# The products of the SSM output projection set among the halves of the paged attention, in a two-layer decoder step

## The chip, the cores and the metric

One NeuronCore of a Trainium2 chip runs the whole kernel. The metric is the time of the device for one execution, in microseconds (us); lower is better. The engines are PE (matmul), with its weight loads shown apart as PEld, DVE (vector), ACT (scalar), POOL (GpSimd) and SP (sync), whose queue issues most of the DMAs here. All data are float32.

## The reference

One inference step of a trunk with two layers: a prompt of 256 tokens and 8 sample tokens, each sample with 2048 tokens of cached context in 16 pages of 128, share the weights. Cut to what matters here, a layer is:

```python
h = rmsnorm(x); proj = h @ w_in         # gates, z, xBC, dt, c_q, c_kv, k_rope
# branch A (SSM): conv, chunked scan, gate with silu(z), grouped norm
ya = rmsnorm_grouped(y * silu(z)) @ w_ssm_proj          # the y projection
# branch B: latent attention; the samples' keys and values come from a page table
kv = cache_latent[l][page_table]; kr = cache_krope[l][page_table]
p  = softmax((q_lat @ kv.T + q_pe @ kr.T) * scale); o = p @ kv
yb = (o @ w_vb) @ w_mla_proj
x = x + (sigmoid(gate_a) * ya + sigmoid(gate_b) * yb) @ w_out
x = x + peer(rmsnorm(x, norm_ffn))      # product-key retrieval of experts
```

The y projection is 264 x 1024 by 1024 x 1024. The prompt's attention is causal, over 2 tiles of 128 tokens, 8 heads.

## The kernel before

A hardware loop runs two layers, each unrolled, with one instruction stream per engine. The order of the work is written out by hand on every engine, and semaphores tie the streams. PSUM is used as two rings of four banks: `wide` (banks 0 to 3, emptied mostly by ACT) and `aux` (4 to 7, emptied by DVE). PE fills banks in program order and DVE reads them in the same order, so both streams must list the pieces alike.

Weights stream through `wring`, two buffers of one block each. `load_block` on SP waits, for block n, until PE has begun block n-1 (semaphore `blocks_begun`), and PE's `next_block` waits for the block's landing. The y projection has 4 blocks of 256 columns (1 MB each); every block gives two outputs m of 128 features by 264 tokens, each a `product` of 8 chunks (L456). DVE multiplies each into `gate` (L1209).

The cached context of a sample comes in two halves of 8 pages, so there are 16 halves (`HALVES`). A page is 272 KB (128 partitions of 544 floats: latent turned, rotary key turned, latent). Three halves are held (`HELD`); slot 2 lies in room that the SSM work uses until `ring_free`. Ahead of the issue of each half, SP loads its eight page numbers from DRAM into registers (`half_numbers`, L1776: one load of the table's address and one of the numbers); `half_pages` (L1783) then issues eight DMAs. From half 3 on SP waits, after it has the numbers, for the values product of the half three before (`marks["values", i - HELD]`).

On PE each half is: `half_scores` (L772 and L776), the pieces of the prompt's attention that `PROMPT_PIECES` sets to this half, `half_turns` (L465, two transposes of the probabilities), `half_values` (L797). Between scores and turns DVE takes the maximum (L1251 to L1254) and ACT the exp (L1653); between turns and values DVE copies (L1259). The prompt's pieces are `prompt_scores(t, q)` (L738, L741), `prompt_turns` (transposed probabilities, copied by DVE into `pt`) and `prompt_values` (L760). DVE's `prompt_maxima` (L1225) and `prompt_probs` (L1233, which scales the probabilities by the sums) stand ahead of what follows them in its order, and ACT's exps of the prompt are set by `PROMPT_EXPS`.

All eight outputs of the y projection stand before half 0 on PE and DVE. On SP their blocks stand so: block 0 before the pages of half 1, block 1 after them and before the wait on `ring_free`, block 2 in the middle of half 2, block 3 after it, then the first block of w_mla, then the pages of halves 3 to 15, then the rest. `pt` lies in the room of `z`, which is also `yt`, the input of the y projection. The row `nrow` (1024 floats in each partition) holds the layer's first norm weight, used once; POOL reloads it with the second one (`norm_ffn`) after the state work, and DVE reads it for the norm ahead of the experts (L1344). POOL also loads and stores the SSM states of the samples (L1874, L1868); ACT scales them (L1626) in the stretch in which the gates' products run and SP issues halves 0 and 1.

## Time and profile before

| | |
|---|---|
| runs, median (lowest to highest of 3) | 2533.2 us (2532.52 to 2535.57) |
| profiled execution, its own time | 2528.51 us |
| its span, first to last instruction | 2527.0 us |
| mean granted TensorE clock | 0.944 of full |
| PE / DVE / ACT / POOL busy | 82% / 60% / 19% / 25% of the span |

The profile is of one execution. A page gives busy times, a span in slices and the costliest groups of instructions; the trace behind it can be asked for a timeline, for windows, for one line's instructions and for waits. A layer takes about half of the span; the page halves are the stretches from 327.75 to 451.40 us (layer 0) and from 1580.60 to 1700.80 us (layer 1). In a timeline, a row is a merged run of one line's instructions: start, length (from the first start to the last end), engine, line, operands, count, and in brackets the idle time of the engine before it and who ended it. PE's records count a product of float32 twice (x16 are eight products).

### The profile page before, as it was taken

The page shows a single profiled execution, that of the slowest core. Times are in us where ns is not written, and L with a number is a line of the kernel's source. Part 1 is how long each engine was busy: PE and PEld are TensorE (multiplying, and loading weights), DVE is VectorE, ACT ScalarE, POOL GpSimd, SP SyncE. Part 2 cuts the span into 40 slices and gives each one's busy share as a digit, 9 for nine tenths or more (in the row PEclk, how much of TensorE's full clock was granted, in tenths as well). Part 3 has the DMA queues.
Part 4 walks back from the last instruction along what each step waited for, and adds up shares of the span by engine and source line. Part 5 has one row for each costly group of instructions (what it writes and reads, how often), then busy time and mean ns, then how long its engine had stood idle before and what let it go on. Part 6 is the DMA issues. An engine that isn't in the chain of part 4 may idle for free. (4 is left out here: it accounts for less than half of the span.)

```text
span 2527.0 us, 26287 instructions
## 1 busy us (share of the span) xinstructions
PE 2067.5 (82%) x8858; PEld 1158.4 (46%) x8858; DVE 1518.1 (60%) x3811; ACT 477.2 (19%) x1458; POOL 633.3 (25%) x592
## 2 busy tenths in 40 slices
PE   6999777888888877787779988779879887777775
PEld 4886554654444322222258866446534343222222
DVE  2534423227878888888525343232387878888884
ACT  1226211001111111111122361110111111111111
POOL 0001000003343444444200010000043444444441
PEclk9999788889999999999979998789899999999998
DMA  5436368129999999999744273762399999999996
GB/s 158 149 97 216 125 222 271 56 82 377 424 422 409 427 385 427 427 427 427 332 146 155 92 237 119 235 227 84 100 425 423 424 412 427 380 427 427 426 425 268
DMA packets 201953, 740.27 MB, mean 293 GB/s; under 512 B 16274, under 2 KB 92490, under 8 KB 133696
## 3 DMA queue, kind: packets, MB, share of 16 engines
q0 software_dynamic: 83008, 581.14, 55.5%
q1 hardware_dynamic: 118800, 157.36, 19.3%
q8 instruction: 72, 1.18, 0.2%
q14 instruction: 73, 0.60, 0.1%
HBM read 727.17 MB, written 11.46 MB: 292 GB/s over the span
## 5 line engine op out<-in xcount | busy, mean ns | idle before, releaser
L915 PE MATMUL ps<-arena 128*128 128x512 f32 (+1 forms) x2112 | 1015.8, 615 | 258.7 <-DVE arena L1447 258.5
L1889 POOL DMA_INDIRECT arena<-in_peer_uv,arena x528 | 587.8, 1113 | 824.1 <-PE ps L915 695.4
L915 PEld LDWEIGHTS ps<-arena 128*128 128x128 f32 (+1 forms) x2112 | 365.6, 187 | 886.0 <-DVE arena L1447 576.8
L1438 DVE CUSTOM_DVE_ANT_0 arena<-arena,h 128x1024 f32<-128x1024 f32 x512 | 626.5, 1224 | 198.8 <-DMA arena<-in_peer_uv,arena 190.5
L456 PE MATMUL ps<-ht_tok,wring 128*128 128x264 f32 x1664 | 391.9, 392 | 6.7 <-DMA wring<-in_w_in 5.1
L456 PEld LDWEIGHTS ps<-ht_tok,wring 128*128 128x128 f32 x1664 | 316.5, 193 | 79.7 <-issue 15.4
L1710 ACT ACTIVATE arena<-arena 128x1 f32<-128x1 f32 x528 | 105.8, 202 | 1035.9 <-DVE arena L1438 1035.3
L1447 DVE TENSOR_SCALAR arena<-consts,arena 128x128 f32<-128x128 f32 (+1 forms) x528 | 181.8, 344 | 42.7 <-ACT arena L1710 42.0
L1880 POOL DMA_DIRECT2D arena<-in_peer_keyst x2 | 1.1, 552 | 539.7 <-PEq L862 539.7
L456 PE MATMUL ps<-arena,wring 128*128 128x264 f32 x384 | 89.7, 396 | 3.7 <-DMA wring<-in_w_ssm_proj 2.6
L456 PE MATMUL ps<-wring,gate 128*128 128x256 f32 (+1 forms) x384 | 87.1, 386 | 6.0 <-DVE gate L1328 6.0
L456 PEld LDWEIGHTS ps<-arena,wring 128*128 128x128 f32 x384 | 74.4, 195 | 18.4 <-DMA wring<-in_w_ssm_proj 3.5
L465 PE MATMUL ps<-consts,h 128*128 128x128 f32 (+2 forms) x166 | 42.6, 356 | 44.4 <-DVE h L1344 18.7
L456 PEld LDWEIGHTS ps<-wring,gate 128*128 128x128 f32 (+1 forms) x384 | 60.0, 160 | 32.9 <-DVE gate L1328 6.8
L465 PE MATMUL ps<-consts,arena 128*128 128x128 f32 (+2 forms) x162 | 31.0, 332 | 45.4 <-DMA arena<-in_ssm_norm 28.8
L772 PE MATMUL ps<-arena 128*32 128x256 f32 x512 | 46.9, 499 | 18.8 <-DMA arena<-in_pages 18.7
L797 PE MATMUL ps<-arena 128*32 128x256 f32 x512 | 41.9, 453 | 24.6 <-DVEq L1261 24.6
L456 PE MATMUL ps<-wring,ht_tok 128*128 128x272 f32 (+5 forms) x288 | 61.0, 372 | 1.1 <-DVE ht_tok L947 1.1
L1868 POOL DMA_DIRECT2D out<-h x16 | 14.2, 887 | 187.7 <-DVE h L1147 187.7
L1333 DVE TENSOR_TENSOR x<-x,ps 128x256 f32<-128x256 f32 (+1 forms) x24 | 10.0, 417 | 78.1 <-PE ps L456 78.1
L465 PEld LDWEIGHTS ps<-consts,h 128*128 128x128 f32 (+2 forms) x166 | 23.8, 173 | 69.0 <-DVE h L1344 19.7
L1147 DVE TENSOR_TENSOR h<-h,arena 128x1024 f32<-128x1024 f32 x16 | 19.6, 1225 | 57.4 <-ACT h L1626 57.4
(297 smaller groups left out, 1875.0 us busy)
## 6 DMA issues: line engine op xcount, KB each, us to landing
arena<-in_pages SPq DMA_DIRECT2D x256, 272.0 KB, 4.2
wring<-in_w_in SPq DMA_DIRECT2D x38, 1024.0 KB, 5.5
wring<-in_peer_wq SPq DMA_DIRECT2D x16, 1024.0 KB, 15.7
arena<-in_peer_uv,arena POOLq DMA_INDIRECT x528, 11.5
h<-in_state_ssm POOLq DMA_DIRECT2D x16, 512.0 KB, 7.2
out<-h POOLq DMA_DIRECT2D x16, 512.0 KB, 6.1
wring<-in_w_ssm_proj SPq DMA_DIRECT2D x8, 1024.0 KB, 8.0
wring<-in_w_out SPq DMA_DIRECT2D x8, 1024.0 KB, 4.9
```

Of the source, the lines that this page charges most:

```text
L456: last = pe.matmul(dst, w(c), rhs(c), start=start and c == 0, stop=stop and c == chunks - 1)
L465: return pe.transpose(dst, src, ident[0:rows, 0:rows])
L772: pe.matmul(ps[32 * g:32 * g + 32, b, 0:256], qs[:, s, c, :], held[:, slot, 2 * g:2 * g + 2, c * P:(c + 1) * P], start=c == 0, stop=False, ...
L797: last = pe.matmul(ps[32 * g:32 * g + 32, b, 0:KV_LORA], pts[:, i % 2, j, g, :], held[:, slot, 2 * g + j, 2 * P + ROPE:KV_ROW], start=j == ...
L915: last = pe.matmul(ps[0:outs, SUM_BANK[t] + half, :], diag[:, n % DIAGS, 0:outs], ring[:, n % RING, D_MODEL + half * 512:D_MODEL + (half + ...
L1147: dve.tensor_tensor(new, new, stx[:, s % 2, :, :], ALU.add).then_inc(sem("state_ready"), 1)
L1333: aux.emptied(dve.tensor_tensor(xs, xs, ps[0:rows, b, 0:BLOCK], ALU.add))
L1438: dve.tensor_tensor_reduce(ring[:, k, 0:D_MODEL], ring[:, k, 0:D_MODEL], tokens, 1.0, 0.0, ALU.mult, ALU.add, dots[:, column(n)]).then_inc ...
L1447: dve.tensor_scalar(diag[:, n % DIAGS, 0:outs], table[:, 0:outs], gel[:, column(n)], wexp[:, column(n)], ALU.mult, ALU.mult).then_inc(sem( ...
L1710: act.activation(gel[:, at:at + 1], dots[:, at:at + 1], ACT.Gelu).then_inc(sem("gelu_ready"), 1)
L1868: pool.dma_start(h1[b], places[b % PLACES]).then_inc(sem(f"state_store{b % PLACES}"), 16)
L1889: pool.indirect_dma_start(ring[:, k, :], None, table, bass.IndirectOffsetOnAxis(ap=idx[:, TOPK * u + j:TOPK * u + j + 1], axis=0)).then_in ...
```

## The change

Each output m of the y projection becomes a piece, `ssm(m)`, and `PROMPT_PIECES` sets outputs 0 to 7 into halves 1, 3, 4, 5, 10, 11, 13 and 14, between the half's scores and its turns, on PE and DVE alike. Some prompt pieces move with it: the second tile's scores go from halves 7 to 10 to halves 6 to 9, the values of the first tile from 8 to 11 to 7 to 10, the four turns of the second tile from 13 and 14 to 12. The second tile's exps come one half earlier.

On SP, weight block 0 comes after the pages of half 1, and blocks 1, 2 and 3 come ahead of halves 5, 8 and 14 (`SSM_LOADS`). Half 2 is issued whole, right after the wait on `ring_free`. The first w_mla block comes after all pages.

Since `yt` is now read through half 14, `pt` moves: its first key chunk into the room of the key weights `wkb` (all read by then), its second one into `nrow`. So POOL reloads `nrow` only once the prompt's last values product is done (`marks["prompt_mixed"]`), and the semaphore `nrow_used` goes. What is computed is the same.

```diff
--- before.py
+++ after.py
@@ -80,15 +80,17 @@
 SAMPLE_QUERIES = TOPK * (P_HEADS - 2) - 8
 
 PROMPT_PIECES = {
-    0: [("scores", (0, 0))], 1: [("scores", (0, 1))], 2: [("scores", (0, 2))], 3: [("scores", (0, 3))], 4: [], 5: [],
-    6: [("turns", (0, 0, 0)), ("turns", (0, 0, 1))], 7: [("scores", (1, 0))], 8: [("scores", (1, 1)), ("values", (0, 0, 0))],
-    9: [("scores", (1, 2)), ("values", (0, 0, 1))], 10: [("scores", (1, 3)), ("values", (0, 1, 0))], 11: [("values", (0, 1, 1))], 12: [],
-    13: [("turns", (1, 0, 0)), ("turns", (1, 0, 1))], 14: [("turns", (1, 1, 0)), ("turns", (1, 1, 1))],
+    0: [("scores", (0, 0))], 1: [("scores", (0, 1)), ("ssm", (0,))], 2: [("scores", (0, 2))], 3: [("scores", (0, 3)), ("ssm", (1,))],
+    4: [("ssm", (2,))], 5: [("ssm", (3,))], 6: [("turns", (0, 0, 0)), ("turns", (0, 0, 1)), ("scores", (1, 0))],
+    7: [("scores", (1, 1)), ("values", (0, 0, 0))], 8: [("scores", (1, 2)), ("values", (0, 0, 1))], 9: [("scores", (1, 3)), ("values", (0, 1, 0))],
+    10: [("ssm", (4,)), ("values", (0, 1, 1))], 11: [("ssm", (5,))], 12: [("turns", (1, 0, 0)), ("turns", (1, 0, 1)), ("turns", (1, 1, 0)), ("turns", (1, 1, 1))],
+    13: [("ssm", (6,))], 14: [("ssm", (7,))],
     15: [("values", (1, 0, 0))], 16: [("values", (1, 0, 1)), ("values", (1, 1, 0)), ("values", (1, 1, 1))],
 }
+SSM_LOADS = {5: 1, 8: 2, 14: 3}
 PROMPT_EXPS = {
     3: [("exp", 0, range(0, 4))], 4: [("exp", 0, range(4, 8))],
-    10: [("exp", 1, range(0, 4))], 11: [("exp", 1, range(4, 8))],
+    9: [("exp", 1, range(0, 4))], 10: [("exp", 1, range(4, 8))],
 }
 
 
@@ -229,7 +231,6 @@
 
 ARENA_ATT, A2 = cut([("qpt", 2 * TOKENS), ("pts", 2 * 256)])
 assert A2 <= ARENA_SSD["z"][0]
-ARENA_ATT["pt"] = ARENA_SSD["z"]
 W1 = share(ARENA_ATT, "wqb", Y1, 3 * 1024)
 assert W1 <= ARENA_SSD["conv"][0] + 6 * CONV_ROW
 E1 = share(ARENA_SSD, "xde", W1, 1024)
@@ -362,7 +363,7 @@
         qnt = mla("qnt").rearrange("p (q t) -> p q t", q=4)
         wqb = mla("wqb").rearrange("p (c n) -> p c n", c=3)
         sc = mla("s").rearrange("p (h t) -> p h t", h=A_HEADS)
-        pt = mla("pt")[:, 0:2048].rearrange("p (k h t) -> p k h t", k=2, h=A_HEADS)
+        pt = [ap.rearrange("p (h t) -> p h t", h=A_HEADS) for ap in (mla("wkb"), nrow[:, :])]
         ot = mla("ot").rearrange("p (c t) -> p c t", c=4)
         obs = hbuf[:, 0:2048].rearrange("p (b r) -> p b r", b=SAMPLES)
         probs = hbuf[:, 2048:2560].rearrange("p (k t) -> p k t", k=2)
@@ -720,12 +721,16 @@
                             last = pe.matmul(ps[32 * g:32 * g + 32, b, hh * SAMPLES:(hh + 1) * SAMPLES], pick, qpt[:, hh // 4, SEQ:TOKENS], start=True, stop=True)
                     aux.filled(last)
 
-                    pe.wait_ge(sem("yt_ready"), 1)
-                    for k in range(4):
-                        w = next_block(DC, BLOCK)
-                        for m in range(2):
-                            b = aux.fill()
-                            aux.filled(product(ps[:, b, 0:TOKENS], lambda c: w[:, c, m * P:(m + 1) * P], lambda c: yt[:, c, :], DC))
+                    def ssm(m):
+
+                        if m == 0:
+                            pe.wait_ge(sem("yt_ready"), 1)
+                        if m % 2 == 0:
+                            state["w"] = next_block(DC, BLOCK)
+                        w = state["w"]
+                        b = aux.fill()
+                        aux.filled(product(ps[:, b, 0:TOKENS], lambda c: w[:, c, (m % 2) * P:(m % 2 + 1) * P], lambda c: yt[:, c, :], DC))
+
 
 
                     def prompt_scores(t, q):
@@ -757,7 +762,7 @@
                             pe.wait_ge(sem("prompt_turned"), t + 1)
                         b = aux.fill()
                         for k in range(t + 1):
-                            last = pe.matmul(ps[:, b, :], lat[:, k, c * P:(c + 1) * P], pt[:, k, 4 * q:4 * q + 4, :], start=k == 0, stop=k == t)
+                            last = pe.matmul(ps[:, b, :], lat[:, k, c * P:(c + 1) * P], pt[k][:, 4 * q:4 * q + 4, :], start=k == 0, stop=k == t)
                         aux.filled(last)
 
                     def half_scores(i):
@@ -804,6 +809,8 @@
                         for piece, at in PROMPT_PIECES[i]:
                             if piece == "scores":
                                 prompt_scores(*at)
+                            elif piece == "ssm":
+                                ssm(*at)
                             elif piece == "turns":
                                 prompt_turns(*at)
                             else:
@@ -822,6 +829,7 @@
                     aux.filled(turn(ps[0:SAMPLES, b, P:2 * P], fin[:, 136:144], P))
                     for piece, at in PROMPT_PIECES[HALVES]:
                         prompt_values(*at)
+                    marks["prompt_mixed"] = aux.n
                     pe.wait_ge(sem("sample_weights"), 1)
                     b = aux.fill()
                     aux.filled(turn(ps[:, b, 0:SAMPLES], fin[0:SAMPLES, 384:512], SAMPLES))
@@ -1024,7 +1032,6 @@
                     last.then_inc(sem("h_ready"), 1)
                     for c in range(DC):
                         copy_out(ht[:, c, :], TOKENS)
-                    dve.nop().then_inc(sem("nrow_used"), 1)
 
 
                     dve.wait_ge(sem("wide_free"), 4 + marks["tail0"])
@@ -1204,10 +1211,10 @@
                     dve.memset(fin[:, 384:512], 0.0)
                     dve.wait_ge(sem("hs_store"), 16)
                     then(dve.memset(mla("pts"), 0.0))
-                    for m in range(DC):
+                    def ssm(m):
+
                         b = aux.read()
                         aux.emptied(dve.tensor_tensor(gate[:, m, :], gate[:, m, :], ps[:, b, 0:TOKENS], ALU.mult))
-
 
                     def prompt_scores(t, q):
 
@@ -1234,7 +1241,7 @@
 
                     def prompt_turns(t, k, q):
 
-                        copy4(pt[:, k, 4 * q:4 * q + 4, :].rearrange("p h t -> p (h t)"))
+                        copy4(pt[k][:, 4 * q:4 * q + 4, :].rearrange("p h t -> p (h t)"))
                         if (k, q) == (t, 1):
                             dve.wait_ge(sem("aux_free"), 4 + aux.n)
                             dve.nop().then_inc(sem("prompt_turned"), 1)
@@ -1278,6 +1285,8 @@
                                 prompt_scores(*at)
                                 if at[1] == 3:
                                     prompt_maxima(at[0])
+                            elif piece == "ssm":
+                                ssm(*at)
                             elif piece == "turns":
                                 if at[1:] == (0, 0):
                                     prompt_probs(at[0])
@@ -1807,20 +1816,17 @@
                     half_pages(0, numbers, range(4, 6))
                     block_of(w_in, GATE_B, 3)
                     half_pages(0, numbers, range(6, 8))
+                    half_pages(1, half_numbers(1))
                     block_of(w_ssm, 0, 0)
-                    half_pages(1, half_numbers(1))
-                    block_of(w_ssm, 0, 1)
                     sp.wait_ge(sem("ring_free"), 1)
-                    numbers = half_numbers(2)
-                    half_pages(2, numbers, range(0, 4))
-                    block_of(w_ssm, 0, 2)
-                    half_pages(2, numbers, range(4, 8))
-                    block_of(w_ssm, 0, 3)
-                    mla_block(0)
+                    half_pages(2, half_numbers(2))
                     for i in range(HELD, HALVES):
+                        if i in SSM_LOADS:
+                            block_of(w_ssm, 0, SSM_LOADS[i])
                         numbers = half_numbers(i)
                         sp.wait_ge(sem("aux_full"), marks["values", i - HELD])
                         half_pages(i, numbers)
+                    mla_block(0)
                     mla_block(1)
                     for k in range(4):
                         block_of(w_out, 0, k)
@@ -1873,7 +1879,7 @@
                             pool.wait_ge(sem("state_used"), b)
                             pool.dma_start(places[place], h0[b - 1 + PLACES]).then_inc(sem(f"state_load{place}"), 16)
 
-                    pool.wait_ge(sem("nrow_used"), 1)
+                    pool.wait_ge(sem("aux_full"), marks["prompt_mixed"])
                     pool.dma_start(nrow[:, :], of_layer("norm_ffn", layer).partition_broadcast(P)).then_inc(sem("ffn_row_load"), 16)
 
                     pool.wait_ge(sem("attention_done"), 1)
```

## Rows read from the trace of the kernel before

**Rows 1.** The page: busy us (share of span) xinstructions of each engine.

```profile
PE 2067.5 (82%) x8858; PEld 1158.4 (46%) x8858; DVE 1518.1 (60%) x3811; ACT 477.2 (19%) x1458; POOL 633.3 (25%) x592
```

**Rows 2.** Timeline of PE ahead of the page halves, layer 0.

```profile
296.10 15.91 PE L456 MATMUL ps<-arena,wring 128*128 128x264 f32 x64
...
313.32 14.51 PE L456 MATMUL ps<-arena,wring 128*128 128x264 f32 x64 [1.30 <-DMA wring<-in_w_ssm_proj]
```

**Rows 3.** Windows over the halves, each layer: busy us, PEclk, DMA share.

```profile
327.75:451.40 123.65, 89.94 (x1190) 53.88 (x1190) 40.16 (x103) 19.02 (x73) 0.00 (x0) 0.82 0.72 236
...
1580.60:1700.80 120.20, 88.62 (x1189) 52.92 (x1189) 40.26 (x103) 19.01 (x73) 0.00 (x0) 0.80 0.74 243
```

**Rows 4.** Timeline of SP's queue, layer 0.

```profile
297.53 0.38 SPq L1752 DMA_DIRECT2D wring<-in_w_ssm_proj  x1
...
301.70 2.07 SPq L1783 DMA_DIRECT2D arena<-in_pages  x4
...
333.47 103.64 SPq L1783 DMA_DIRECT2D arena<-in_pages  x104
...
432.76 0.34 SPq L1783 DMA_DIRECT2D arena<-in_pages  x1
```

**Rows 5.** SP's table loads, 333 to 443 us (ns min/median/max); issues.

```profile
L1776 SPq TENSOR_LOAD <-in_page_table_ptr x12: 1674/2458/2935, 338.3 to 429.0; - x12
...
L1776 SPq TENSOR_LOAD <-in_page_table x12: 874/878/939, 340.6 to 431.7; - x12
...
335.02 2.06 SPq L1783 DMA_DIRECT2D arena<-in_pages  x4
```

**Rows 6.** Timeline of PE in the halves; last, group of prompt turns.

```profile
333.00 1.05 PE L772 MATMUL ps<-arena 128*32 128x256 f32 x16
...
337.90 1.05 PE L772 MATMUL ps<-arena 128*32 128x256 f32 x16
...
385.13 1.05 PE L772 MATMUL ps<-arena 128*32 128x256 f32 x16
...
392.53 1.07 PE L772 MATMUL ps<-arena 128*32 128x256 f32 x16
...
419.01 1.05 PE L772 MATMUL ps<-arena 128*32 128x256 f32 x16
...
421.84 0.44 PE L465 MATMUL ps<-consts,h 128*128 128x128 f32 x2 [1.33 <-ACT h L1653]
...
422.66 1.07 PE L797 MATMUL ps<-arena 128*32 128x256 f32 x16 [0.38 <-DVEq L1261]
...
443.23 1.94 PE L772 MATMUL ps<-arena 128*32 128x256 f32 x16 [2.33 <-DMA arena<-in_pages]
...
1662.46 1.93 PE L797 MATMUL ps<-arena 128*32 128x256 f32 x16 [2.88 <-DVEq L1261]
...
1695.53 1.07 PE L772 MATMUL ps<-arena 128*32 128x256 f32 x16
...
L465 PE MATMUL ps<-consts,arena 128*128 128x128 f32 x24 | 4.0, 321 | 5.5 <-DVE arena L1233 5.5
```

**Rows 7.** Timeline of DVE around the y products, both layers.

```profile
296.58 1.34 DVE L1193 MEMSET arena<- 128x1536 f32 x1 [0.48 <-issue]
...
299.37 0.17 DVE L1204 MEMSET h<- 128x128 f32 x1 [0.31 <-DVE arena L1198]
...
304.93 0.43 DVE L1209 TENSOR_TENSOR gate<-gate,ps 128x264 f32<-128x264 f32 x1 [3.06 <-PE ps L456]
...
1549.50 1.34 DVE L1193 MEMSET arena<- 128x1536 f32 x1 [0.48 <-issue]
```

**Rows 8.** SP's table loads, half 1; timeline of ACT, layer 0.

```profile
L1776 SPq TENSOR_LOAD <-in_page_table_ptr x1: 971/971/971, 238.1 to 238.1; - x1
...
L1776 SPq TENSOR_LOAD <-in_page_table x1: 3958/3958/3958, 239.2 to 239.2; - x1
...
252.94 2.44 ACT L1626 ACTIVATE h<-h,exs 128x128 f32<-128x128 f32 x8 [4.50 <-DMA h<-in_state_ssm]
```

## The prediction

> **What bounds the kernel now.** I read the page first, for the shares: PE is busy 82% of the span and no engine is solid [rows 1], so the limit has to be found stage by stage. The PE timeline around the moved work comes next: the 64 products of the y projection (two records each) stand alone from 296.10 us to 327.75 us, right ahead of the first page half [rows 2]. Then the windows over the sixteen halves: 123.65 us in layer 0 and 120.20 us in layer 1, with PE busy 90 and 89 us of them at a mean granted clock of about 0.8, DMA share 0.72 to 0.74 [rows 3]. So PE has gaps there, and neither it nor the DMA engines fill the stage. The chain of waits on the page names only the last few instructions and tells nothing here.
>
> The queue of SP explains the gaps. It issues the first refill (half 3) at 333.47, released by the values of half 0, and the last one (half 15) at 432.76; that is 99.29 us for twelve steps, 8.27 us each, whatever PE had in the half [rows 4]. One step is: load the address of the page table (median 2.46 us) and the eight page numbers (0.88 us), together 3.3 us and serial on SP, then eight DMA issues at four in 2.06 us, so 0.57 us apart and about 4.9 us with the first's own work [rows 5]. SP waits for PE only once per layer. The last pages are read by PE at 443.23, 10.47 us after their first issue [rows 4, 6]. **So the stage is paced by SP's serial step, and its end is the start of that series plus thirteen steps, plus landing, plus one half.** The series starts late because PE reaches half 0 only after the y products.
>
> **The change, part by part.**
>
> *Products moved.* The eight y outputs leave 296.1 to 327.75 and go one each into halves 1, 3, 4, 5, 10, 11, 13, 14. One costs 3.56 us of PE (DVE's cadence on them, 0.43 us work and 3.13 us wait) [rows 7]. Inside a half an output stands between the page scores and the turn of the page probabilities, where PE waits 1.33 us for DVE and ACT in a half without a piece [rows 6], so it adds only 2.23 us there; the DVE multiply of 0.43 us runs beside the turn.
>
> *Start.* Half 0 now needs only the masked queries, whose last DVE step ends just before the memset at 299.37 [rows 7]. PE loses 3.3 us against the y products' start and starts half 0 at 299.4.
>
> *SP series.* The load of half 2's pages no longer stands behind the second y block (issued 297.53, waiting for the first y product) but only behind the DVE signal just ahead of the memset at 296.58 [rows 4, 7]. From the end of that block issue, 297.91, to the first pages at 301.70 is 3.8 us, so half 2 begins at 296.6 + 3.8 = 300.4. Half 3 follows at 308.7 (the values of half 0, ready by about 305, no longer hold it). Half 15 is thirteen steps later: 300.4 + 13 x 8.27 = 407.9. To that come three weight blocks in the queue. The issue of one is 0.38 us [rows 4], some 0.6 us with its register work; with its 1 MB ahead of SP's next table loads these may be slower. The same pair of loads behind one block took 3.8 us once and 4.9 us once (the 0.97 and 3.96 us of half 1) [rows 4, 8]. I take 1.0 us a block, bounds 0.6 and 2.2: half 15's first issue at 410.9 (409.7 to 414.5). Blocks 0 and 1 of the buffer are long read when SP asks for them: block 2 wants an output of half 4 when SP is at half 8, block 3 one of half 10 at half 14. No new wait of SP there. Blocks 1 and 3 do come just ahead of their readers in halves 4 and 13; with a 1 MB transfer behind the pages of that half PE may wait about 2 us in each, which costs SP nothing, since it is three halves ahead.
>
> *End.* 410.9 + 10.4 landing = 421.3, then half 15, 8.2 us when it fell at the low clock (443.23 to 451.40) and 5.3 us at the high one (1695.53 to 1700.80) [rows 3, 6]; I take 6.7. End 428.0 against 451.4: 23.4 us.
>
> *Can PE follow?* The time of each half, from one page score to the next, at the high clock: bare 4.54 (419.01 to 422.66, plus 0.89 until the next scores start); with a scores piece of the first tile 4.90; with one of the second tile and a values piece 7.40; with the row maxima of the second tile as well the wait is 2.88 in place of 0.75, so 9.53 [rows 6]. With a y output 4.54 - 1.33 + 3.56 = 6.77, beside a scores piece 4.90 + 3.56 = 8.46. The values piece is about 1.05 of the 4.19 that the two pieces add to 3.21 (1024 of 4096 columns), the scores 3.14. Halves 6 and 12 have the prompt turns: 5.5 us of waits for the normalising and 4.0 us for 24 turns in both together [rows 6], so 2 x 3.21 + 5.5 + 4.0 + 3.14 (the scores piece now in half 6) = 19.1. Sum: 4.90 + 8.46 + 4.90 + 8.46 for halves 0 to 3, 2 x 6.77 for 4 and 5, 19.1 for 6 and 12, 2 x 7.40 for 7 and 8, 9.53 for 9, 7.82 for 10, 3 x 6.77 for 11, 13 and 14, 5.3 for 15: 117.1. From 299.4 PE would end at 416.5 if all were at 2.4 GHz. It won't be: the first 32 of these y products took 15.91 us where the next 32 took 14.51, the clock still coming back from the wait ahead of them [rows 2]; half 0 with its gaps will be low, and later in the loop page scores at 443.23 took 1.93 us for 1.05 [rows 6]. I put 3 us on the start and 5 on the rest (bounds 1.4 and 20): 424.5. That is 3.5 us under SP's 428, so SP still sets the end, narrowly; a delay of one can hide in the other.
>
> *Layer 1.* The DVE memset that marks the start stands at the same place relative to the y products (1549.50 against 296.58), so half 2 starts at 1549.5 + 3.8 = 1553.3, half 15 at 1553.3 + 107.5 + 3.0 = 1663.8, the end is 1663.8 + 10.4 + 6.7 = 1680.9 against 1700.8: 19.9 us.
>
> *Page half 1 ahead of block 0.* SP formerly issued w_ssm block 0, loaded the page numbers of half 1 from 238.1 on and then its pages [rows 8]; now half 1 goes out some 9 us earlier (it no longer waits with the block for the last gate block to be begun) and block 0 behind. Both run beside the state loads. ACT waits 4.50 us for one of these at 252.94 [rows 8], and the chain to the start of the y products goes through it. Pages that are over sooner help the last two state loads and hurt the one before. I take nothing, bounds -4 and +3 us a layer.
>
> *The rest.* Turned probabilities go to the key weights (last read ahead of the loop) and to the norm row; same copies, same bytes. The load of the second norm row moves from the end of the state work to just after the loop. It is read only after all of the w_mla and w_out products, which cover it; if they didn't, its whole landing would be paid. On POOL only the load of the keys stands behind it, and that waits for the end of attention anyway. The exps of tile 1 come a half earlier, still behind their maxima. The load of the first w_mla block moves behind the pages, at about 416; it is used some 20 us after the loop. After the loop everything hangs on the loop's end by PE, DVE and ACT alone, so the gain is carried through. Gates, state work and the expert stage are untouched: nothing.
>
> **Sum.** 23.4 + 19.9 = 43.3 us off the profiled run of 2528.5 us: 2485.2. The median of the runs shown, 2533.2, lies 4.7 above it: 2489.9, given as 2490.
>
> A rule of the Trainium skill bears on SP's step. The row gives 2.46 us for the load of one address and 0.88 us for eight numbers in this stage [rows 5]; the page "Runtime: NRT & Kernel Launch", section "Instruction fetch mechanics", gives about 200 ns a register, an estimate of under 2 us for the pair. By that SP's step would be some 1.3 us shorter and PE's 424.5 would end the loop, 2483 us in all; the measurement decides for 3.3. The page "DMA: Bandwidth & Descriptors", section "Latency and other measured facts", has HBM access at 0.2 us on average and 2 us at high load, which speaks for slower table loads when weight blocks join the pages; the two rows for these loads, 3.3 and 4.9 us, agree.
>
> **Rivals.** (1) PE takes over: the low clock covers more of the loop, or table waits and gaps add up. Of the 117.1 us some 22 are waits (5.5, 2.88 and about 0.9 a half), so 95 are work. If a quarter of it is low, the chain is 117.1 + 24 = 141, its end 436 to 441 as gaps hide some of it, gain 10 to 15 us a layer, 2533.2 - 27 = 2506. For it: the clock of 0.8 in the loop now. Against: less idle than now. (2) SP and PE both better: 1.3 us of a state load saved, blocks at 0.6 us, last half high: 428 becomes 424, 2478. (3) No change: something behind the loop holds the end. I see no transfer or wait with a time of its own there. (4) Slower: PE, with the y outputs now among its gaps, at the low clock through the whole loop. It decides once the chain from half 0 on is over 152 us (451.4 - 299.4), that is over 34 us added, a third of the work at half speed; with all of it low, 117.1 + 95 = 212 us, 60 us more a layer, about 2653. Against it: unbroken stretches (an output is 3.56 us) bring the clock back, as in rows 2.
>
> **How the numbers follow.** Forecast 0.62 (own range 2482 to 2499), rival 1 0.20, rival 2 0.11, rival 3 0.03, rival 4 0.04. The range 2475 to 2512 takes in the forecast, rival 2 and most of rival 1. A change of 0.2% is about what a measurement of this kernel can tell. Faster 0.93, same 0.03, slower 0.04.
>
> **What would show it.** Page issues from about 300 to 416 in steps of 8.3 us without a wait for PE, half 0 at 299 to 300, the loop's end near 428, PE's clock over the loop above 0.85, page waits of PE still there in the late halves. Wrong if SP waits for values of PE, if steps are over 9 us, or if the time before 296 moved.

## The result, and the profile after

The changed kernel took 2489.5 us (median of 4 runs, 2487.38 to 2492.25) against 2533.6 us for the kernel before: a ratio of 0.9835 with a 95% interval of 0.9821 to 0.985. The forecast was 2490.0. The profiled execution took 2492.25 us with a span of 2490.7, that is 36.3 us less than the 2527.0 of before; the forecast, made against that same execution, was 43.3 us less. So the time was met more closely than the gain in the trace: the profiled run of before lay 5.1 us below the median of its runs, that of after lies 2.7 us above its own. In a second set of runs of the same kernel (below) the gain was 45.0 us by the medians and 46.8 us by the spans of the profiled executions. Profiles of one kernel thus differ by more than the forecast was off, and what follows sets the second profile beside the first where it matters.

The page after, its first part and its groups for the page scores and the values (line, engine, operation, tiles, count, busy us and mean ns, idle before and its releaser):

```profile
PE 2056.9 (83%) x8858; PEld 1156.7 (46%) x8858; DVE 1516.7 (61%) x3811; ACT 477.6 (19%) x1458; POOL 633.6 (25%) x592
...
L1883 POOL DMA_DIRECT2D nrow<-in_norm_ffn x2 | 1.1, 564 | 345.4 <-PE ps L765 345.4
...
L802 PE MATMUL ps<-arena 128*32 128x256 f32 x512 | 36.9, 408 | 23.8 <-DVEq L1268 23.8
...
L777 PE MATMUL ps<-arena 128*32 128x256 f32 x512 | 38.9, 428 | 15.7 <-DMA arena<-in_pages 9.7
```

The shares hardly moved. The second line is the load of the norm row at its new place: POOL waits for it a long time, and nobody waits for POOL. The last line is the one that tells something: PE still waits for pages, 9.7 us in both layers together. The windows over the sixteen halves (length, then busy us of PE, weight loads, DVE, ACT and POOL, granted clock, DMA share, GB/s) answer to [rows 3]:

```profile
298.46:427.69 129.23, 107.20 (x1317) 74.26 (x1318) 43.20 (x112) 19.02 (x73) 0.00 (x0) 0.95 0.84 276
1532.05:1663.44 131.39, 109.46 (x1316) 75.37 (x1317) 43.27 (x112) 19.02 (x73) 0.00 (x0) 0.93 0.82 271
```

The halves became 5.6 and 11.2 us longer (4.0 and 8.1 in the second profile), and they now hold the y products, which stood alone for 31.65 us before [rows 2]. PE is busier in them (107 us for 90), its clock rose from 0.82 and 0.80 to 0.95 and 0.93, and the DMA share from 0.72 and 0.74 to 0.84 and 0.82. The queue of SP in layer 0 answers to [rows 4]:

```profile
297.48 21.59 SPq L1792 DMA_DIRECT2D arena<-in_pages  x24
319.27 0.38 SPq L1761 DMA_DIRECT2D wring<-in_w_ssm_proj  x1
325.10 21.83 SPq L1792 DMA_DIRECT2D arena<-in_pages  x24
347.11 0.38 SPq L1761 DMA_DIRECT2D wring<-in_w_ssm_proj  x1
352.35 47.08 SPq L1792 DMA_DIRECT2D arena<-in_pages  x48
399.62 0.39 SPq L1761 DMA_DIRECT2D wring<-in_w_ssm_proj  x1
405.18 13.09 SPq L1792 DMA_DIRECT2D arena<-in_pages  x16
```

Each group is three, six or two halves of eight pages. Between the groups stand the weight blocks, and behind each block the next pages come 4.9 to 5.5 us after its issue is over (319.65 to 325.10, 347.49 to 352.35, 400.01 to 405.18), where between two halves without a block it is about 3.4 (steps of 8.4 less the 5.0 of eight issues). The first halves and the last as PE ran them (start, duration, line, tile, count, and in brackets the idle time before and its releaser):

```profile
294.42 1.04 PE L721 MATMUL ps<-arena,consts 128*32 128x8 f32 x64 [5.93 <-DVE arena L1183]
298.46 1.94 PE L777 MATMUL ps<-arena 128*32 128x256 f32 x16 [3.00 <-DVEq L1208]
...
305.01 1.05 PE L777 MATMUL ps<-arena 128*32 128x256 f32 x16
...
327.01 1.05 PE L777 MATMUL ps<-arena 128*32 128x256 f32 x16
327.88 0.63 PE L781 MATMUL ps<-arena 128*32 128x64 f32 x32
328.44 3.83 PE L457 MATMUL ps<-arena,wring 128*128 128x264 f32 x16
332.10 0.38 PE L466 MATMUL ps<-consts,h 128*128 128x128 f32 x2
332.98 1.07 PE L802 MATMUL ps<-arena 128*32 128x256 f32 x16 [0.49 <-DVEq L1268]
334.03 1.07 PE L777 MATMUL ps<-arena 128*32 128x256 f32 x16
...
422.40 1.07 PE L777 MATMUL ps<-arena 128*32 128x256 f32 x16 [1.29 <-DMA arena<-in_pages]
...
427.69 0.39 PE L822 MATMUL ps<-arena,latt 128*8 128x64 f32 x4
```

Half 4 (327.01 to 334.03) shows a y output in a half: its eight products (16 records, 3.83 us) stand between the page scores (L777, L781) and the turns of the probabilities (L466), whose wait is gone. The last half begins after a wait for its pages, which had been issued from 413.12 on, and the loop ends at 427.69, where before it ended at 451.37.

The stretch from the pick of the queries (L721, before L720) to the loop's end is the measure for the rest of this text; I call it the loop stretch. It was 156.24 us in layer 0 and 152.77 in layer 1, and is 133.27 and 135.44: 22.97 and 17.33 us less, 40.3 together. What lies ahead of layer 0's pick took 0.7 us less and what lies ahead of layer 1's 2.1 more; the two expert stages took 0.7 and 1.2 less; the stretch from the loop's end to the first gather took 2.3 us more in each layer, 127.9 and 127.8 us for 125.6 and 125.5. That makes 36.3. What lies outside the loop stretch moves by as much from one execution to the next: in a second execution of the same kernel layer 0's pick was reached at 290.36 and not 294.42, and the stretches to the first gather took 125.9 and 125.7 us. So the 2.3 us a layer are no steady part of the change, and I read nothing from what lies outside.

### The profile page after: what moved, and what is told of

It is laid out like the page before. It is cut to its first block and busy times, and to the rows that moved or that the text cites. A ratio compares the mean times of both kernels' runs of the same rounds, so it can differ in the third digit from the quotient of the medians.

```text
span 2490.7 us, 26285 instructions
## 1 busy us (share of the span) xinstructions
PE 2056.9 (83%) x8858; PEld 1156.7 (46%) x8858; DVE 1516.7 (61%) x3811; ACT 477.6 (19%) x1458; POOL 633.6 (25%) x592
## 5 line engine op out<-in xcount | busy, mean ns | idle before, releaser
L466 PE MATMUL ps<-consts,h 128*128 128x128 f32 (+2 forms) x166 | 41.0, 346 | 33.5 <-DVE h L1353 18.7
L466 PE MATMUL ps<-consts,arena 128*128 128x128 f32 (+2 forms) x162 | 29.3, 321 | 45.8 <-DMA arena<-in_ssm_norm 29.1
L802 PE MATMUL ps<-arena 128*32 128x256 f32 x512 | 36.9, 408 | 23.8 <-DVEq L1268 23.8
L777 PE MATMUL ps<-arena 128*32 128x256 f32 x512 | 38.9, 428 | 15.7 <-DMA arena<-in_pages 9.7
L457 PEld LDWEIGHTS ps<-wring,ht_tok 128*128 128x128 f32 (+1 forms) x288 | 43.5, 165 | 17.7 <-issue 2.6
```

The costliest lines, as they stand in the source:

```text
L457: last = pe.matmul(dst, w(c), rhs(c), start=start and c == 0, stop=stop and c == chunks - 1)
L466: return pe.transpose(dst, src, ident[0:rows, 0:rows])
L777: pe.matmul(ps[32 * g:32 * g + 32, b, 0:256], qs[:, s, c, :], held[:, slot, 2 * g:2 * g + 2, c * P:(c + 1) * P], start=c == 0, stop=False, ...
L802: last = pe.matmul(ps[32 * g:32 * g + 32, b, 0:KV_LORA], pts[:, i % 2, j, g, :], held[:, slot, 2 * g + j, 2 * P + ROPE:KV_ROW], start=j == ...
```

## The experiments

My theory was the one on record: the halves are paced by SP, which loads an address and eight page numbers for each half one after the other and then issues eight transfers; the y products fit in under that, so the gain is the earlier start of the series less what the weight blocks cost in the queue. The rivals were that PE itself paces the new loop, that the gain comes from something else that the change does (the turned probabilities, the order of page half 1 and block 0), or that moving the products anywhere would have done.

**Shorter y products.** Each output multiplies two of its eight chunks; waits and loads are the same.

```
-  aux.filled(product(ps[:, b, 0:TOKENS], ..., lambda c: yt[:, c, :], DC))
+  aux.filled(product(ps[:, b, 0:TOKENS], ..., lambda c: yt[:, c, :], 2))
```

> The changed kernel with each y output summed over 2 chunks of 8 instead of 8; the other three quarters of the products are left out, so PE does 21 us less in the page halves of a layer. If SP's series of page loads sets the end of the halves, they end at most 3 us earlier a layer (PE's share is the slow first halves of the second layer and small gaps): 2483 to 2491 us. If PE's chain through the halves set it (the gain coming from gaps that PE fills), 15 us or more a layer would go: under 2460.

Measured: 2484.9 us, ratio 0.9813 (0.9771 to 0.9854), loop stretches 129.66 and 133.53 us. Of products that take 28.75 us alone (next experiment) three quarters were gone, and the loop stretch became 3.6 and 1.9 us shorter; against the second profile of the changed kernel (131.67 and 132.37) it is 2.0 shorter and 1.2 longer. The total can't be told from that of the changed kernel. Where the rest went, the group of page scores on the page of this kernel shows in part:

```profile
L777 PE MATMUL ps<-arena 128*32 128x256 f32 x512 | 43.9, 472 | 26.1 <-DMA arena<-in_pages 20.1
```

PE's wait for pages went from 9.7 us to 20.1: it arrives sooner at pages that aren't there. The other part is the clock. In layer 0's halves PE was busy 95.75 us for 107.20, 11.5 less where some 21 us of products are gone, as the granted clock there fell from 0.95 to 0.84. Both parts say the same: what PE is spared does not shorten the loop. PE doesn't pace the changed loop.

**Products right behind the loop.** All eight outputs after half 15, their three later blocks behind the last pages.

```
-    0: [("scores", (0, 0))], 1: [("scores", (0, 1)), ("ssm", (0,))], ...
+    0: [("scores", (0, 0))], 1: [("scores", (0, 1))], ...      (no "ssm" piece in any half)
-SSM_LOADS = {5: 1, 8: 2, 14: 3}
+SSM_LOADS = {}
+                    for m in range(DC):          # PE and DVE, behind the last half
+                        ssm(m)
```

> The changed kernel with all eight y outputs after half 15, their blocks 1 to 3 loaded after the pages; page series and halves start as early as in the changed kernel. If the outputs gained by lying in the time in which PE waits for SP, that is lost: halves end near 420 us, plus 29 us of outputs, so 449 to 452 against 451.4 before: 2524 to 2534 us. If the earlier page series alone brought the gain, about 2490.

Measured: 2539.2 us, ratio 1.0026 (1.0008 to 1.0044), a little above the kernel before and above the 2524 to 2534 that I had expected. The ten runs lie in two groups, four from 2531.0 to 2533.9 and six from 2538.9 to 2542.5; the profile is of a run of the first, so what makes the others slower stays open. PE at the end of layer 0's halves:

```profile
419.62 1.07 PE L802 MATMUL ps<-arena 128*32 128x256 f32 x16 [0.73 <-DVEq L1270]
420.62 28.75 PE L457 MATMUL ps<-arena,wring 128*128 128x264 f32 x128
449.29 0.39 PE L824 MATMUL ps<-arena,latt 128*8 128x64 f32 x4
```

The halves end at 420.62, 30.8 us earlier than before, but the 64 products (128 records) then take 28.75 us alone. So starting the pages early is worth nothing by itself: the gain is that the products have SP's time as cover. The run also gives the loop without any products and blocks in it: 126.2 us from the pick, against 133.3 and 131.7 with all of them in the two profiles of the changed kernel. Eight outputs and three blocks cost 5.5 to 7.1 us there, where the outputs alone take 28.75.

**The turned probabilities alone.** The kernel before with `pt` in the room of the key weights and the norm row, and the later load of that row.

```
-ARENA_ATT["pt"] = ARENA_SSD["z"]
-        pt = mla("pt")[:, 0:2048].rearrange("p (k h t) -> p k h t", k=2, h=A_HEADS)
+        pt = [ap.rearrange("p (h t) -> p h t", h=A_HEADS) for ap in (mla("wkb"), nrow[:, :])]
```

> The kernel before with one part of the change alone: the turned prompt probabilities in the key weights' room and the norm row, and the second norm row loaded after the prompt's last values. Order of products and loads as before. If this part costs and brings nothing: 2531 to 2536 us. If the later norm row or the other places cost something: over 2538; if they are part of the gain: under 2529.

Measured: 2529.9 us, ratio 0.9988 (0.9972 to 1.0005). No effect that ten runs can tell.

**Page numbers ahead of the weight block.** In the steps with a block, the table loads go first, then the block, then the pages.

```
                     for i in range(HELD, HALVES):
+                        numbers = half_numbers(i)
                         if i in SSM_LOADS:
                             block_of(w_ssm, 0, SSM_LOADS[i])
-                        numbers = half_numbers(i)
```

> The changed kernel with SP's two table loads of halves 5, 8 and 14 ahead of the weight block instead of behind it. A step of SP with a block took 10.1 to 11.1 us against 8.2 without. If the address load is slow because the block's 1 MB is queued ahead of it, those steps fall to about 8.8 and SP's last issue comes 5 to 6 us earlier a layer, of which PE lets some 3 through: 2480 to 2486 us. If the block costs the same wherever it stands (the DMA engines are the limit): 2488 to 2491.

Measured: 2487.7 us, ratio 0.9827 (0.9786 to 0.9868), loop stretches 130.90 and 131.14. The total lies between the two ranges that I had named and can't be told from that of the changed kernel; the queue can. First the changed kernel's loads of the page-table address in layer 0 (durations in ns, least, median, most; first and last start), all of them and the one behind block 1, then the same loads in this experiment and its queue around block 1:

```profile
L1785 SPq TENSOR_LOAD <-in_page_table_ptr x13: 2025/2532/4202, 301.8 to 409.5; - x13
...
L1785 SPq TENSOR_LOAD <-in_page_table_ptr x1: 4202/4202/4202, 319.7 to 319.7; - x1
```

```profile
L1785 SPq TENSOR_LOAD <-in_page_table_ptr x13: 1507/2270/3264, 301.7 to 405.0; - x13
```

```profile
297.38 21.56 SPq L1792 DMA_DIRECT2D arena<-in_pages  x24
322.07 0.39 SPq L1761 DMA_DIRECT2D wring<-in_w_ssm_proj  x1
322.69 21.95 SPq L1792 DMA_DIRECT2D arena<-in_pages  x24
```

Behind the megabyte of the block the address took 4.20 us, 1.67 more than the median (2.93 to 4.50 us behind the six blocks of both layers); with the block behind the loads none took over 3.27 in this layer, and the pages follow the block 0.62 us after its start. Half 5 begins 2.4 us sooner (322.69 for 325.10). But some of the slowness moves to the next loads, which now stand behind the block and eight pages: 2.39, 3.26 and 1.74 us in layer 0 and 2.70, 3.68 and 3.39 in layer 1. From half 2's first page to half 15's, SP took 110.63 and 113.27 us, where the two profiles of the changed kernel have 115.64 and 113.73 in layer 0 and 117.47 and 114.64 in layer 1. So a slow address load is part of what a block costs in the queue, the order wins back 1.4 to 5 us of the series rather than the 5 to 6 expected, and what of it reaches the time of the kernel is not shown.

**The change again**, in one set of runs with the next two kernels and with the early first output further down.

> The changed kernel as it is, on the chip of the three runs that follow, so that these can be set against it and not only against the kernel before. 2485 to 2492 us, 0.982 to 0.985 of before.

Measured: 2486.9 us, ratio 0.9828 (0.9811 to 0.9844), loop stretches 131.67 and 132.37. It shows how far two profiles of one kernel differ: 1.6 and 3.1 us in the loop stretch, and 10.5 us in the span.

**The kernel before without the table loads.** Halves 3 to 15 are loaded with the page numbers of half 2; all else is the kernel before.

```
                     for i in range(HELD, HALVES):
-                        numbers = half_numbers(i)
```

> The kernel before, with SP's two table loads left out for halves 3 to 15: these read the pages of half 2's numbers again, so the data are other ones, the transfers as many and as large. If SP's serial step (loads 3.3 us, issues 4.9) paces the halves, the step falls to what the next limit allows: 6.7 us for 2.2 MB at the 330 GB/s that the DMA engines' busy share implies, or PE's own chain, some 102 us from half 0; the halves end 16 to 20 us earlier a layer: 2494 to 2501 us. If the DMA engines or landing pace the halves, 2528 to 2536.

Measured: 2499.7 us, ratio 0.9878 (0.9858 to 0.9898). The halves took 103.0 us (326.78 to 429.79) in place of 123.65 and 102.9 in place of 120.20. SP's waits (who, for whom, us in total, times, longest) in layer 0 and in layer 1, and then the one of layer 1 in the kernel before:

```profile
SPq L1783 <- PE ps L797: 38.0, 12, 11.5
...
SPq L1783 <- PE ps L797: 37.0, 12, 11.5
...
SPq L1783 <- PE ps L797: 7.8, 1, 7.8
```

SP now waits for PE's values in 12 of 13 refills, 38.0 us in all, where before it did so once. The transfers themselves are not quicker for reading the same pages again: from issue to landing they took 4.6 us in the median, where they took 4.1 before. This is the clearest proof that SP's serial step was the pace of the kernel before: without the loads of numbers the halves become 20.7 and 17.3 us shorter, and then PE is the bound.

**Numbers of two halves in one pair of loads.** The kernel with the change, and SP loads the sixteen numbers of a sample at once, at every even half (`sample_numbers`, new, is `half_numbers` over 16 entries).

```
+                    both = sample_numbers(1)        # 16 numbers, one address
+                    half_pages(2, both)
                     for i in range(HELD, HALVES):
-                        numbers = half_numbers(i)
+                        if i % 2 == 0:
+                            both = sample_numbers(i // 2)
-                        half_pages(i, numbers)
+                        half_pages(i, both[HALF_PAGES * (i % 2):])
```

> The changed kernel with one pair of table loads for both halves of a sample (16 numbers) from half 2 on, so odd halves have no loads; the result is the same. SP's mean step falls by about 1.6 us, the series would end 20 us earlier. If PE's chain of 117 us plus its slow clock stands 3 to 5 us under SP's end, as forecast, only that much is gained a layer: 2480 to 2486 us. If PE's chain were much shorter than worked out, 2465 or less; if the DMA engines limit, 2488 to 2492.

Measured: 2482.6 us, ratio 0.9804 (0.9785 to 0.9822), loop stretches 127.49 and 124.53. PE's waits for pages are gone from the list of waits, and SP waits for PE:

```profile
SPq L1798 <- PE ps L802: 10.4, 6, 5.0
```

Here PE sets the loop, and its chain can be read: 123.5 us in layer 0 (299.66 to 423.11) and 120.5 in layer 1 (1531.57 to 1652.06). Not all of that reaches the total. The loop stretches are 12.0 us shorter in sum than those of the change again, from the same set of runs, but the medians differ by 4.4 us, and outside the loops, in stages that the edit doesn't touch, the profile here is 13 us longer. Run a second time beside the last two kernels below:

> The changed kernel with one pair of table loads per sample again, to stand beside the next run on its chip. 2479 to 2485 us, 0.979 to 0.982 of before.

Measured: 2479.3 us, ratio 0.9796 (0.9778 to 0.9813), loop stretches 124.66 and 124.65.

**First y output ahead of half 0.** To see what the slow clock of half 0 costs, output 0 stands ahead of the halves.

```
-    0: [("scores", (0, 0))], 1: [("scores", (0, 1)), ("ssm", (0,))], ...
+    0: [("scores", (0, 0))], 1: [("scores", (0, 1))], ...
+                    ssm(0)                          # PE and DVE, ahead of the loop
```

> The changed kernel with y output 0 ahead of half 0 instead of in half 1. PE stood idle for 3 us there and ran half 0, in the second layer half 1 too, at 1.2 GHz; SP waited 4.7 us in the second layer for the values of halves 0 and 1. If PE's slow start costs as those waits say, 1 to 4 us go: 2485 to 2489, the gain in the second layer. If SP's series from its own start sets the end regardless: no difference from the change as it is.

Measured: 2490.8 us, ratio 0.9832 (0.9808 to 0.9855), loop stretches 131.74 and 131.49. PE at the start of layer 0's halves:

```profile
296.44 5.56 PE L457 MATMUL ps<-arena,wring 128*128 128x264 f32 x16
301.93 1.07 PE L777 MATMUL ps<-arena 128*32 128x256 f32 x16
```

The output itself took 5.56 us for 3.83, partly at the lower clock, and the page scores behind it 1.07 us where they took 1.94 before: the slow stretch has moved into the output. The waits of SP for PE that I wanted to remove are not there to be removed. They were 0.2 and 4.7 us in the first profile of the changed kernel, nothing in either layer of the second, and 0.9 and 1.2 us here. The loop stretches are those of the change again (131.67 and 132.37), and the medians, 2490.8 (2482.0 to 2494.6) and 2486.9 (2481.8 to 2488.9), can't be told apart: SP paces the rest.

**Block 0 ahead of page half 1**, as before the change.

```
-                    half_pages(1, half_numbers(1))
                     block_of(w_ssm, 0, 0)
+                    half_pages(1, half_numbers(1))
```

> The changed kernel with one part undone: y weight block 0 ahead of the pages of half 1, as before. The forecast took nothing for this part, with 3 to 4 us a layer either way. In the first layer the y stage began 0.7 us earlier with the change and 1.9 us later in the second beyond what came from the layer ahead. If the part is worth nothing: 2485 to 2491, like the change as it is. If page half 1 beside the state loads helped or hurt by the bounds: 2 to 8 us off that.

Measured: 2489.2 us, ratio 0.9829 (0.9813 to 0.9845), loop stretches 132.70 and 134.23. ACT's waits for the state loads ahead of the loop are 9.8 and 9.5 us with the old order and 9.6 and 9.2 with the new. The order of these two is worth nothing that these runs can tell.

**Outputs where PE waits anyway.** On top of the paired numbers, outputs 3, 4 and 5 go from halves 5, 10 and 11 into 6, 9 and 12, the halves in which PE waits for DVE, and DVE makes the prompt's probabilities ahead of their pieces.

```
-    4: [("ssm", (2,))], 5: [("ssm", (3,))], 6: [("turns", (0, 0, 0)), ...
+    4: [("ssm", (2,))], 5: [], 6: [("ssm", (3,)), ("turns", (0, 0, 0)), ...
-    9: [("scores", (1, 3)), ("values", (0, 1, 0))],
+    9: [("scores", (1, 3)), ("ssm", (4,)), ("values", (0, 1, 0))],
-    10: [("ssm", (4,)), ("values", (0, 1, 1))], 11: [("ssm", (5,))], 12: [("turns", (1, 0, 0)), ...
+    10: [("values", (0, 1, 1))], 11: [], 12: [("ssm", (5,)), ("turns", (1, 0, 0)), ...
```

> With the loads per sample PE waits for no page, so its own chain of 120 to 123 us sets the end. Here three outputs lie where PE waits longest for DVE: output 3 ahead of the turns in half 6 (2.1 us), 4 ahead of the values in half 9 (2.9), 5 ahead of the turns in half 12 (3.2); DVE normalises ahead of them. If PE's chain is the limit now, each hides the difference to the 1.3 us it hid before: 0.8 + 1.5 + 1.9, some 4 us a layer: 2474 to 2479 us. If SP or the DMA engines are the limit: no difference from the run beside it.

Measured: 2474.3 us, ratio 0.9782 (0.9766 to 0.9797): the lowest median of all, 5.0 us below the paired numbers alone in the same set of runs. The five runs of each overlap (2470.5 to 2478.6 and 2473.8 to 2481.9), so the 5.0 us are not clear of the spread. PE's wait for DVE ahead of the values, first in the changed kernel and then here, layer 0:

```profile
PE ps L802 <- DVEq L1268: 12.2, 16, 2.9
```

```profile
PE ps L803 <- DVEq L1269: 9.5, 16, 1.5
```

The longest of the sixteen waits fell from 2.9 us to 1.5, and the waits of the turns for DVE, 5.3 us, are gone too. But in the profiled executions the loop stretch is 124.75 and 123.79 us against 124.66 and 124.65, that is 0.8 us less in all: PE waits for ACT (3.9 us) and for pages (1.3 us) in their place, and the clock takes the rest. PE's idle time in the halves fell by 2.8 us a layer (20.5 to 17.7 in layer 0), but its busy time rose from 103.1 to 106.0 and 105.0 us, at a granted clock of 0.95 and 0.96 for 0.97: the page scores of halves 6 and 12 take 1.94 us, where they took 1.05. The median lies in the range that I had expected, but not for my reason. The 4 us a layer are not in the loops, and whether the 5.0 us lie in the spread between executions or in a stage that I haven't found stays open.

## Why the prediction was right

**What bounds it.** Right, and shown from three sides: products cut to a quarter give back at most 3.6 us of the loop stretch, and the rest turns into page waits and a lower clock; the table loads taken away give 20.7 and 17.3 us of the halves and turn SP's free queue into a waiting one; half as many address loads give 4 to 11 us of the loop stretch, by which two profiles are set side by side. The signs named beforehand came too: issues from 297.5 to 413 us in steps of 8.4 (those with a block apart), the loop's end at 427.7, a clock above 0.85, page waits in the late halves. One sign against showed in layer 1 alone (below).

**The start.** Half 0 was put at 299.4 and began at 298.46, half 2's pages at 300.4 and went out at 297.48. The 3.8 us between the end of a block's issue and the first pages was the row that I took for the start; in it lay an address load of the common length (2.19 us), while this one took 0.8 us; 0.7 us more is that the pick came earlier than in the profile of before. Term too large by 2.9 us.

**The series.** Thirteen steps and three blocks were put at 107.5 + 3.0 = 110.5 us and took 115.6 (297.48 to 413.12). The plain steps were right: 8.4 us on average for 8.27. The three with a block took 11.1, 10.6 and 10.1, so a block costs 2.2 us over the plain steps beside it and 2.3 over 8.27. **This is the step that was mis-sized**: I had taken 1.0, inside bounds of 0.6 and 2.2, and it came out at the upper bound or just over it. The second profile gives 2.2 us too (steps of 10.4, 10.9 and 9.9 beside plain ones of 8.25), and against the loop without blocks (108.48 us for the thirteen steps) it is 1.8 to 2.4. The pair of loads behind block 0, 0.97 us for the address and 3.96 for the numbers [rows 8], was the right neighbour: 4.9 us for a common 3.3. Behind the twelve blocks of the two profiles the pair took 4.2 to 5.4 us; I had stayed nearer to the other case of 3.8.

**The end.** Landing took 9.3 us for 10.4, and the last half 5.3 for 6.7, as it fell at the high clock. Together with the start these made up for the blocks: 428.0 - 2.9 + 5.1 - 1.1 - 1.4 = 427.7. The 428.0 on record was met to 0.3 us by terms of which four were off by one to five. The mechanism was right; that the end was met so closely is luck, and in the second profile it came at 422.0, with a pick 4.1 us earlier.

**PE's chain.** Put at 117.1 us at the high clock and 8 for the low one, 125 in all. Where SP doesn't pace, it was 123.5 and 120.5, and 120.6 in both layers of the second profile of the paired numbers. A bare half with an output took 6.85 us in most places (7.02 in the half 4 shown) for 6.77. The low clock was priced too high: 120.6 for 117.1 leaves 3.5 us of the 8, most of it in halves 0, 9 and 10 (6.5, 10.2 and 8.9 us for 4.90, 9.53 and 7.82). So the rival by which PE takes over (2506 us) and that by which it stays at the low clock throughout (2653) fell; the clock went to 0.95 and 0.93, as the argument against them had it: fewer gaps, not more. The halves of the changed kernel took 127.6 to 131.4 us in its two profiles, so PE's chain was 4 to 11 us under them, rather than the 3.5 that I had put.

**Layer 1.** Here 132.9 us was the forecast for the loop stretch and 135.4 the time. I had written that SP would meet no new wait for PE. In this execution it did (issues, SP's wait, PE in halves 0 and 1):

```profile
1531.07 25.04 SPq L1792 DMA_DIRECT2D arena<-in_pages  x24
```

```profile
SPq L1792 <- PE ps L802: 4.7, 2, 2.3
```

```profile
1532.05 1.94 PE L777 MATMUL ps<-arena 128*32 128x256 f32 x16 [3.00 <-DVEq L1208]
...
1538.98 1.93 PE L802 MATMUL ps<-arena 128*32 128x256 f32 x16 [0.38 <-DVEq L1268]
1540.69 1.93 PE L777 MATMUL ps<-arena 128*32 128x256 f32 x16
```

The first three halves' issues take 25.04 us for 21.59 in layer 0. Half 0 lay wholly at 1.2 GHz (granted clock 0.50 from 1532 to 1541) and took 8.6 us (1532.05 to 1540.69; 6.55 in layer 0), half 1 began at that level too, and SP, which started sooner than forecast, waited for the values of both, 4.7 us in two waits. I had priced the slow clock on PE's chain and not on SP's first two refills, which hang on it.

It is this execution and not the layer or the change. The same stretch in the second profile of the same kernel, layer 1:

```profile
1526.33 1.93 PE L777 MATMUL ps<-arena 128*32 128x256 f32 x16 [3.00 <-DVEq L1208]
...
1531.95 1.07 PE L802 MATMUL ps<-arena 128*32 128x256 f32 x16 [0.37 <-DVEq L1268]
1532.84 1.05 PE L777 MATMUL ps<-arena 128*32 128x256 f32 x16
```

The scores of half 0 stand at the lower level here too, but its values at the higher one. Half 0 took 6.5 us, as it did within 0.2 us in both layers of the seven other profiles that begin the loop with the same half. SP waited here for no values, and the loop stretch was 132.37 us, against the forecast of 132.9. Why the clock came back later once is not shown.

**What was put at nothing.** The turned probabilities and the norm row (ratio 0.9988) and the order of half 1 and block 0 (0.2 and 0.3 us of state waits) are nothing that these runs can tell, as forecast. After the loop the gain was carried through but for 2.3 us a layer in the first profile, which the second one doesn't show (0.3 and 0.2 us).

The Trainium skill, "Runtime: NRT & Kernel Launch", section "Instruction fetch mechanics", puts a register load at about 200 ns. For the eight numbers this trace agrees in kind (0.88 us, 110 ns each), for the address it doesn't: it took 0.8 to 4.5 us, and the whole case goes by the measurement. The Trainium skill, "DMA: Bandwidth & Descriptors", section "Latency and other measured facts", gives memory access at high load as ten times that of the average; the address load behind a weight block, 2.9 to 4.5 us for a median of 2.4 to 2.5, points the same way.

## What to carry to other kernels

Where neither TensorE nor the DMA engines fill a loop, read the queue that issues its transfers as an engine of its own: if its issues come at even steps whatever the compute had in between, its serial work is the pace, and products that stand alone elsewhere fit in under it. A register load of an address is then a cost to be shared among as many transfers as can be; a large transfer in the same queue may slow that load, and with the load put first some of the slowness moved to the next one. Ask also what hangs on the first piece behind a gap: here the page scores behind 3 us of idle time ran at the lower clock (1.94 us for 1.05) in both profiles of the changed kernel. And take a second profile before a difference of a few us is explained: 4.7 us of waits in the first one here were absent from the second.

## What the runs showed of the hardware

- In the first profile of the changed kernel, in the loop stretches, the load of one address by SP took from 0.8 us (the first behind a wait of SP of 54 us) over a median of 2.5 to 4.5 us (right behind a 1 MB transfer), while eight numbers took 0.88 us in the median (3.96 at most, behind a block in the kernel before); sixteen in one load took 1.69 in the median (3.84 at most).
- Serial loads in SP's queue alone made the halves of the kernel before a fifth longer (123.65 for 103.0 us), at a DMA share of 0.72.
- With the gaps of a loop filled, TensorE's granted clock rose from 0.82 and 0.80 to 0.95 and 0.93 of full speed over it, so that products which take 28.75 us alone at full speed added only 17 and 21 us to PE's busy time there (107 and 109 for 90 and 89). The other way round, three quarters of these products taken out again brought the clock down to 0.84 in layer 0 and gave back 11.5 us of busy time.
